# A hybrid decoder trunk on one core: the samples' attention and decays' sums in the norms' rounds, half of the attention's projection ahead of the scan, and tile 1's first two query blocks alone

## What is computed

```
h = RMSNorm(x) * (1 + scale) + shift            # scale, shift: from c @ w_ada (6 vectors of 1024 per sequence)
parts = h @ w_in                                # q, k, v | conv input | decay, beta | z | gate_a, gate_b
A: sliding-window attention (window 128, 8 heads of 64, 2 kv heads, sinks, bias) -> @ w_att_out
B: q, k, v = silu(conv4(...)); q, k = l2norm(q), l2norm(k)       # 4 heads of 128
   g = -exp(a_log) * softplus(decay + dt_bias); beta = sigmoid(...)
   delta rule with decay exp(g), chunk by chunk (128 tokens), gated RMSNorm with silu(z) -> @ w_delta_out
y = sigmoid(gate_a) * A + sigmoid(gate_b) * B;   x += gate1 * RMSNorm(y @ w_out)
h2 = RMSNorm(x) * (1 + scale2) + shift2
query = h2 @ w_query                            # 8 heads x 2 halves of 128
scores against 128 sub keys per half, top 16 of each, top 16 of the 256 sums -> 16 experts of 16384
f = sum over experts of gate * gelu(h2 . u_e) * v_e;   x += gate2 * RMSNorm(f)
```

## Time and profile before

| | |
|---|---|
| median of 3 runs | 1865.48 us (1865.09 to 1865.55) |
| profiled execution | 1861.27 us, of which the span of the trace 1859.5 us |
| TensorE clock granted, mean | 0.83 of full |
| busy: TensorE, VectorE, ScalarE, GpSimd | 1447.3, 1248.9, 704.1, 611.3 us |
| read from memory | 640.84 MB, 348 GB/s over the span |
| gathers | 520, first dot product at 468 us |
| TensorE, VectorE busy from 250 to 462 us | 196.4, 160.0 us |

### The profile page before, as it was taken

One profiled execution on the slowest core, in us unless ns is written; L12 is line 12 of the kernel. 1 busy time (PEld: TensorE's weight loads), 2 busy tenths in 40 slices (PEclk: granted clock), 3 DMA queues, 4 the chain that ended last, 5 costly groups with the idle time before them and its releaser, 6 DMA issues.

```text
span 1859.5 us, 23227 instructions
## 1 busy us (share of the span) xinstructions
PE 1447.3 (78%) x8298; PEld 684.0 (37%) x8298; DVE 1248.9 (67%) x2827; ACT 704.1 (38%) x1799; POOL 611.3 (33%) x590
## 2 busy tenths in 40 slices
PE   8999988999888889689776666666666676667666
PEld 4777877887454446444222111101111110001001
DVE  3077678776866665776767666777667677667665
ACT  3145472213545553935324222432222243222223
POOL 1100000000543323333445444454444444444442
PEclk9999998999999999899988767867766676665666
DMA  9533362126999999999999999999999999999997
GB/s 348 179 121 118 129 241 80 35 80 219 417 421 419 422 414 405 401 342 394 413 420 423 425 424 424 425 424 425 424 424 423 421 423 417 422 421 418 423 422 305
DMA packets 101059, 647.54 MB, mean 348 GB/s; under 512 B 11858, under 2 KB 12026, under 8 KB 32933
## 3 DMA queue, kind: packets, MB, share of 16 engines
q0 software_dynamic: 76912, 555.82, 72.3%
q1 hardware_dynamic: 23840, 90.16, 13.3%
q10 hardware_dynamic: 192, 0.09, 0.0%
HBM read 640.84 MB, written 6.18 MB: 348 GB/s over the span
## 4 chain that ended last, share of the span: by engine, by line
PE 38%; DMA 38%; DVE 9%; ACT 9%; issue 5%; POOL 1%; ACTq 0%; SPq 0%; DVEq 0%; POOLq 0%
DMA arena<-in_euv,consts 37%; PE abank L926 23%; PE dbank L1654 4%; PE dbank L926 4%; DVE arena L2390 3%; PE fsum L1654 2%; PE fsum L1648 2%; ACT consts L892 2%; ACT L890 2%; ACT small L890 1%; ACT L795 1%; DMA arena<-in_wstream 1%; PE fsum L990 1%; POOL arena L480 1%; PE abank L1538 1%
## 5 line engine op out<-in xcount | busy, mean ns | idle before, releaser
L2390 DVE CUSTOM_DVE_ANT_0 arena<-arena 128x1024 f32<-128x1024 f32 x520 | 632.8, 1223 | 387.6 <-DMA arena<-in_euv,consts 386.7
L480 POOL DMA_INDIRECT arena<-in_euv,consts x520 | 577.0, 1110 | 784.3 <-PE dbank L1654 335.5
L926 PE MATMUL abank<-arena 128*128 128x128 f32 (+4 forms) x2456 | 555.1, 383 | 19.5 <-ACT arena L497 6.9
L1654 PE MATMUL dbank<-arena,consts 128*32 128x512 f32 x1024 | 364.5, 850 | 202.2 <-ACT consts L892 201.9
L926 PEld LDWEIGHTS abank<-arena 128*128 128x128 f32 (+1 forms) x2456 | 393.0, 191 | 176.0 <-issue 65.4
L890 ACT ACTIVATE small<-small 128x1 f32<-128x1 f32 x520 | 104.7, 201 | 639.5 <-DVE small L2390 632.9
L1654 PE MATMUL fsum<-arena,consts 128*32 128x512 f32 x512 | 191.2, 873 | 113.9 <-ACT consts L892 113.3
L1654 PEld LDWEIGHTS dbank<-arena,consts 128*32 128x32 f32 x1024 | 42.4, 124 | 487.9 <-ACT consts L892 475.9
L497 ACT ACTIVATE arena<-abank 128x512 f32<-128x512 f32 (+5 forms) x237 | 116.0, 489 | 253.2 <-PE abank L926 240.0
L892 ACT ACTIVATE consts<-arena,small 128x32 f32<-128x32 f32 x520 | 167.1, 321 | 16.9
L1654 PEld LDWEIGHTS fsum<-arena,consts 128*32 128x32 f32 x512 | 21.6, 126 | 263.5 <-ACT consts L892 261.0
(11 more groups left out here) (338 smaller groups left out, 1196.1 us busy)
## 6 DMA issues: line engine op xcount, KB each, us to landing
arena<-in_wstream SPq DMA_DIRECT2D x140, 512.0 KB, 6.2
arena<-in_euv,consts POOLq DMA_INDIRECT x520, 13.2
arena<-in_wout SPq DMA_DIRECT2D x8, 1024.0 KB, 8.8
arena<-in_x SPq DMA_DIRECT2D x5, 512.0 KB, 6.8
arena<-in_sdel POOLq DMA_DIRECT2D x1, 2048.0 KB, 9.1
out_deltas<-arena POOLq DMA_DIRECT2D x1, 2048.0 KB, 12.0
out_yp<-arena SPq DMA_DIRECT2D x4, 512.0 KB
arena<-mod SPq DMA_DIRECT2D x3, 512.0 KB, 10.0
```

Of the source, the lines that this page charges most:

```text
L480: pool.indirect_dma_start(ring[n % SLOTS], None, I["euv"], bass.IndirectOffsetOnAxis(cur[:, u % 2, c:c + 1], 0)).then_inc(ring_in[n % SLOT ...
L926: return pe.matmul(out, lhsT, rhs, start=first, stop=last)
L1654: last = pe.matmul(out[e][to:to + 32, :], weighed, v, start=h == 0 and kk == 0, stop=h == PH - 1 and kk == 3, skip_group_check=True)
L2390: TTR(uh, uh, rep[j] if t < NT else h2sb, 1.0, 0.0, ALU.mult, ALU.add, dot[:, n // NQ % 2, n % NQ:n % NQ + 1]).then_inc(s.dots_done, 1)
```

## The change

It has three parts, and some places that follow from them.

1. Rounds of the norms. `AHEAD` puts three ada blocks in each of the first four rounds and none in the other four. The samples' attention, which stood behind the rounds, is a function `own_attention(m)` of the rounds on TensorE and ScalarE, and its VectorE steps, those of g and the remaining modulation stand in the rounds too. The samples' bias and logits are added in the bank (two products into one) instead of on VectorE. ScalarE makes beta ahead of the rounds.
2. Start of the scan. Two of the four gates left stand right behind the rounds, the other two ahead of decays 1 and 2. Two of the four attended blocks (`N_EARLY`) stand ahead of decays 2 and 3, the other two in levels 2 and 3. VectorE's product of E1 with the triangle is gone in each chunk (the later masks hold it). `mgt` lies elsewhere, so it doesn't wait until the modulation has been written out.
3. Stream. Tile 1 is the first of the later tiles in norm and transpose, then the samples; mixing begins a tick later, norms and transposes two. Query blocks 0 and 1 are done for tile 1 alone, 128 columns, at ticks 51 and 52 (`ALONE`), between the transposes of the samples, of tile 2 and of tile 3. Their columns for the other tiles are done at ticks 76 and 79 with the same blocks loaded a second time, so SyncE's last run of loads has 18 instead of 16 blocks.

The diff, cut to its core:

```diff
-BEHIND, AHEAD = [5, 1, 1, 1] + [1] * B_CONV, [1, 2] * DH
+BEHIND, AHEAD = [5, 1, 1, 1] + [1] * B_CONV, [3] * DH + [0] * DH
 GATES = [("z", m) for m in range(B_Z)] + [("a", m) for m in range(B_GA)] + [("b", m) for m in range(B_GB)]
 ROUNDS = [1, 1, 2, 2, 2, 2, 2, 2]
+N_EARLY = 2
...
-        LATER = [NT, 1, 2, 3]
+        LATER = [1, NT, 2, 3]
...
-        MIX_FROM = 34
+        MIX_FROM = 35
         OD_AT = {3: (0,), 4: (1,), 5: (2, 3), 6: (4,), 7: (5, 6), 8: (7,)}
-        GATE_AT = {i: g for g, i in enumerate((9, 11, 13, 15, 17, 18, 20, 21, 23, 24, 26, 27, 29, 30, 32, 33))}
-        FIRST_AT = {i: PH + m for m, i in enumerate((8, 10, 12, 14, 16, 19, 22, 25))}
-        NORMAL = {45: 0, 46: 1, 47: 2, 48: 3}
-        SECOND = {47: 0, 48: 1, 49: 2, 50: 3}
-        TURN = {48: 0, 49: 1, 50: 2, 51: 3}
-        ROWS_LATER = {53: 1, 55: 2, 57: 3}
-        QUERY_AT = (52, 53, 54, 55, 57, 58, 59, 62, 64, 67, 70, 73, 76, 79, 82, 85)
-        QUERY = {i: m for m, i in enumerate(QUERY_AT)}
-
-        SPREAD = {36: (0, 1), 39: (2, 3), 42: (4, 5), 44: (8,), 56: (6, 7)}
+        GATE_AT = {i: g for g, i in enumerate((9, 11, 13, 15, 17, 18, 20, 21, 23, 25, 26, 28, 29, 31, 32, 34))}
+        FIRST_AT = {i: PH + m for m, i in enumerate((8, 10, 12, 14, 16, 19, 22, 24))}
+        NORMAL = {47: 0, 48: 1, 49: 2, 50: 3}
+        SECOND = {49: 0, 50: 1, 51: 2, 52: 3}
+        TURN = {50: 0, 51: 1, 52: 2, 53: 3}
+        ROWS_LATER = {54: 1, 56: 2, 58: 3}
+        ALONE = {51: 0, 52: 1}
+        QUERY_AT = (54, 55, 57, 58, 59, 62, 65, 68, 71, 74, 76, 79, 83, 86, 89, 92)
+        QUERY = dict(zip(QUERY_AT, list(range(2, 12)) + [0, 1] + list(range(12, 2 * PH))))
+
+        SPREAD = {37: (0, 1), 40: (2, 3), 43: (4, 5), 47: (8,), 63: (6, 7)}
...
-            if QUERY.get(i - 1) == 1:
+            if ALONE.get(i - 1) == 1:
...
-        STREAM = list(range(N_QRY + 8)) + BETWEEN + list(range(N_QRY, N_QRY + B_QRY))
+        STREAM = list(range(N_QRY + 8)) + BETWEEN + [N_QRY + m for m in [0, 1] + list(QUERY.values())]
...
+            act.wait_ge(s.cols_in, 48)
+            step(A(ealog, cols[:, K_ALOG:K_ALOG + 4], ACT.Exp))
+            act.wait_ge(s.gx_ready, 1)
+            step(A(gtmp2, gtmp, ACT.Abs))
+            step(A(gtmp2, gtmp2, ACT.Exp, scale=-1.0))
+            step(A(gtmp2, gtmp2, ACT.Ln, bias=ones[:, 0:1]))
+            step(A(beta, nat[:, :, 260:264], ACT.Sigmoid), s.beta_ready)
...
+            def own_attention(m):
+
+                if m == 1:
+                    for i in range(2):
+                        empty(probT[:, 4 * i:4 * i + 4, :])
+                    act.sem_inc(s.kTs_ready, 1)
+                if m == 2:
+                    for kv in range(2):
+                        empty(lt64.rearrange("p (q v g) -> p q v g", v=2, g=HG)[:, :, kv, :], slice(0, NB * HG), scale=HD ** -0.5)
+                    act.sem_inc(s.lt_ready, 1)
+                if m == 3:
+                    empty(prob[0:64, 0, 0:P], slice(0, P), slice(0, 64))
+                    act.sem_inc(s.own_ready, 1)
+                if m == 5:
+                    act.wait_ge(s.nm_ready, NT + 1)
+                    step(A(prob[0:64, 0, 0:P], prob[0:64, 0, 0:P], ACT.Exp, bias=nm8[0:64, 0:1], accum_out=sm8[0:64, 0:1]))
+                    step(A(es8[0:64, 0:1], es8[0:64, 0:1], ACT.Exp), s.exp_done)
+                if m == 6:
+                    empty(ex, slice(0, 48), func=ACT.Exp)
+                    act.sem_inc(s.ex_ready, 1)
+                if m == 7:
+                    empty(lt64, slice(0, 64))
+                    act.sem_inc(s.lt_ready, 1)
+
             for m in range(2 * DH):
                 if m >= 2:
                     act.wait_ge(s.l2_done, m - 1)
...
+            act.sem_inc(s.att_done, 1)
             act.wait_ge(s.mrows_ready, 8)
             for ch in range(NT):
-                if ch == 2:
-                    b = aring.to_read()
-                    step(A(attT[:, :, SEQ:TOK], b[:, 0:32].rearrange("p (b g) -> p g b", g=HG), ACT.Copy), s.aring_free)
-                    act.sem_inc(s.att_done, 1)
+                if ch in (1, 2):
+                    gates(1)
+                if ch >= NT - N_EARLY:
+                    others_attended(ch - NT + N_EARLY)
...
+            def own_attention(m):
+
+                if m == 1:
+                    pe.wait_ge(s.keyc_in, 16)
+                    for i in range(2):
+                        b = aring.to_fill()
+                        for e in range(4):
+                            last = pe.transpose(b[:, e * P:(e + 1) * P], keyc[:, 4 * i + e, :], ident)
+                        last.then_inc(s.aring_full, 1)
+                if m == 2:
+                    pe.wait_ge(s.kTs_ready, 1)
+                    for kv in range(2):
+                        half = slice(64 * kv, 64 * kv + 64)
+                        b = aring.to_fill()
+                        for q in range(NB):
+                            last = mm(b[:, q * HG:(q + 1) * HG], probT[half, q, :], qT[half, :, SEQ + q])
+                        last.then_inc(s.aring_full, 1)
+                if m == 3:
+                    b = aring.to_fill()
+                    mm(b[0:64, 0:P], rels[:, :], onehot[:, P:2 * P], True, False)
+                    pe.wait_ge(s.lt_ready, 1)
+                    mm(b[0:64, 0:P], lt64, ident, False, True).then_inc(s.aring_full, 1)
+                if m == 6:
+                    pe.wait_ge(s.g_ready, 1)
+                    b = aring.to_fill()
+                    for i, tri in enumerate((le, gt, ones)):
+                        last = mm(b[:, 16 * i:16 * i + 16], tri, gg[:, 0:NT, :])
+                    last.then_inc(s.aring_full, 1)
+                if m == 7:
+                    pe.wait_ge(s.prob_ready, NT + 1)
+                    b = aring.to_fill()
+                    pe.transpose(b[:, 0:64], prob[0:64, 0, 0:P], consts[0:64, 0:64]).then_inc(s.aring_full, 1)
+
...
+            keys_and_values(2)
+            keys_and_values(3)
+            for ch in range(NT):
+                if ch in (1, 2):
+                    gate()
+                if ch >= NT - N_EARLY:
+                    pe.wait_ge(s.att_done, 1)
+                    attended()
+                decays(ch)
...
+            def query_begin(m):
+                lo = P if m < 2 else 0
...
+                if i in ALONE:
+                    pe.wait_ge(s.h2T_ready, 2)
+                    project(h2T[1], ((0, P),))
...
-            for n in range(N_AGAIN + 4, N_AGAIN + B_QRY):
+            for n in range(N_AGAIN + 4, N_AGAIN + B_QRY + 2):
...
-                if m == 1:
-                    for c in range(4, 8):
+                if m in (1, 2, 4, 5):
+                    for c in range(*{1: (4, 6), 2: (6, 8), 4: (8, 10), 5: (10, 12)}[m]):
                         modulation(c)
+                if m == 3:
+                    dve.wait_ge(s.beta_ready, 1)
+                    step(STT(gg, gtmp, 0.0, gtmp2, ALU.max, ALU.add))
+                    step(STT(gg, gg, -1.0, bc(ealog, 1, NT + 1), ALU.mult, ALU.mult), s.g_ready)
+                if m == 4:
+                    dve.wait_ge(s.own_ready, 1)
+                    step(dve.tensor_reduce(mx, q0, AX.X, ALU.max))
+                    step(TT(mx, mx, sink, ALU.max))
+                    step(TT(es, sink, mx, ALU.subtract))
+                    step(TS(nm, mx, -1.0, None, ALU.mult), s.nm_ready)
+                if m == 6:
+                    dve.wait_ge(s.exp_done, NT + 1)
+                    step(TT(sm_, sm_, es, ALU.add))
+                    step(recip(sm_, sm_))
+                    step(TS(q0, q0, sm_, None, ALU.mult), s.prob_ready)
                 if m >= 1:
                     dve.wait_ge(s.rn_ready, m)
...
-                step(TT(e1, e1, bc(gt, 1, DH), ALU.mult))
...
+            if N_EARLY == 2:
+                attended(0)
+            decays(2)
...
+            if N_EARLY:
+                attended(N_EARLY - 1)
```

157 lines of the change are left out of this document (47 added, 110 removed).

## The result

The changed kernel took **1891.55 us** (median of 4 runs, 1889.68 to 1895.73), the kernel before 1865.28 beside it (4 runs): 1.0152 of before, 95% interval 1.0136 to 1.0168. It is slower by some 26 to 28 us, where 8 us faster was forecast, and outside the range (to 1868). The profiled execution of the changed kernel took 1895.73 us (span 1893.9), that of before 1861.27; the two profiles differ by 34.5 us, 8 more than the medians.

What follows compares the result with a forecast made beforehand. It took a chain of engines to bound the first quarter and a stream of 520 gathered blocks the rest. Front -3 and stream -5 took 1865.5 to 1857.5 us; range 1849 to 1868.

Steps and rivals of the forecast that it cites:

- Rounds, "3.8 us later": Rounds of norms: VectorE begins keys and values at 279.9, not 276.12, so 3.8 us later.
- the rival: Slower: TensorE's clock halves after idle spells in rounds 6, 7 and levels 4, 5; two halvings +12, 1869.5 us; chance 0.13.
- The replay: Queues ahead of the stream replayed with durations from the profile's rows; it put the start of keys and values at 279.9.
- the chain for beta, costed at 0.5: ScalarE's 5.2 us for beta, moved ahead of round 1, costs 0.5 us, since TensorE is in a gate of 7.2.
- Decays, "+4.0 at this point, 3.8 of it there already": Start of the scan: last mask at 323.6, second products of level 1 4.0 us later, 3.8 of it from the rounds.
- Levels, "-6.1 to -7.0": Merge levels 4 and 5 without attended blocks: 2.3 to 3.2 us off level 4, 3.8 off level 5.
- Table loads, taken at 1.28 without a drain: ScalarE's five added loads in rounds and decays take 1.28 us each; a drain would cost 7 us more.
- Stream, "-7.5 + 2.5 = -5.0": Gathered blocks: 7.5 us back from the wait for tile 1's first scores, 2.5 for two blocks fetched again; net -5.0.
- the hole: Stream at 800 to 860 us: 344 GB/s against 423, 11.2 us lost, 7.5 of them expected back.
- Gates and first queries up to one tick later ... nothing: Stream: these later places cost nothing, the DMA being the bound there; without cover, one gate of 5.6 us late.
- the queries keep TensorE the bound: Rival for the stream: first scores no sooner, or queries behind them keep TensorE the bound; 1865 us; chance 0.2.
- wrong-if clauses: Prediction is wrong if the first dot product comes after 468 us, or the stretch of the queries stays under 360 GB/s.

Runs made afterwards that it cites:

- Front alone: The kernel before with the change's parts ahead of the stream only, its stream as before: 1877.6 us, 1.0072 of before.
- stream alone: The kernel before with the change's stream part only, its front as before: 1874.6 us, 1.0056 of before.
- the rounds as before: Change's front, stream of before, all four attended blocks in levels 2 to 5, modulation blocks spread over all eight rounds as before: 1869.5 us, 1.0020.
- Filled: Change's front with both early attended blocks, stream of before, plus five matmuls nobody reads in levels 4 and 5: 1878.1 us, 1.0062 of before.
- the version without the shift: Kernel before plus tile 1's first two query blocks alone and two more weight blocks, ticks of before, each tile's own wait: 1860.0 us, 0.9973.

## Why the prediction was wrong, step by step

In the changed kernel's own profile the front's terms came out as +13.4 for the rounds (forecast +3.8), +0.8 for the decays (+0.2) and -2.6 for the levels (-6.1 to -7.0), 11.8 in all with what follows, where -3.0 was forecast.

- **Rounds, "3.8 us later"**: mis-sized; 13.4 in this profile (289.51 less 276.12). Front alone has 10.4 against a profile of before's front that starts as early as its own (284.92 less 274.50, of stream alone). Of the rest 2.5 is a gate at the lower clock behind an idle spell of 2.94, which was in the rival, not in the sum; front alone has the same spell, but its clock stayed at 1.00 and its gate took 3.73. The loss stands in the middle: 16.8 us from the third reciprocal to the fourth, where before has 5.2, front alone 16.7, and the rounds as before 16.3, so it is not the modulation. The replay took the samples' scores, which stand there, at half of the earlier trace rows's 3.58, for the clock: front alone has them at 3.31 with the clock at 1.00. The logits came 5.3 later than forecast. And the chain for beta, costed at 0.5, moved the first norm by 5.9. What each of these is worth by itself no run separates.
- **Decays, "+4.0 at this point, 3.8 of it there already"**: right as a difference. 14.2 at the second products of level 1 against 13.4 at the start of keys and values; VectorE idle 5.84 where some 6 were forecast. But the difference hid the price. The prediction has both ends of it: VectorE's own work would be done at 314.4, and with the two blocks ahead the last mask is at 323.6. These 9.2 us, 10 as measured, were never set against the 6.1 to 7.0 for which they were paid; by the prediction's own figures the move was a loss. (The 318.8 that it compares with is misread: the row runs from 318.13 to 321.0. Work taken away had more to give than it counted.)
- **Levels, "-6.1 to -7.0"**: the step that I called the surest, and wrong. The changed kernel gave 2.6. Front alone gave 3.1 in level 4 (15.2 between merges for 18.3), of which 1.6 was before's own dip of the clock, and level 5 and its last merge took back all but 0.8. The sum was VectorE's own, but the block that went was what kept TensorE busy; its first products at half the clock then paced VectorE. Filled, the levels give 5.8, and 4.1 against a profile of before's front without a dip. The error was to leave the clock to a rival while the sum assumed it held, and to take one profile of before for its usual time.
- **Table loads, taken at 1.28 without a drain**: right. In front alone a load at 264.95 is followed by its activation at 266.25. The Trainium skill (ScalarE: Activation LUTs, What ACT_TABLE_LOAD costs) would add some 1.38 to each; no run here shows it.
- **Stream, "-7.5 + 2.5 = -5.0"**: right in size for what it costed, -5.2, but only in the version without the shift. There the hole closes as said, by 9.8 where 7.5 were forecast, and 4.5 are lost ahead of it that were not costed; that the sum fits is in part luck. What failed is the sentence that the rest lies where the DMA is the bound: "Gates and first queries up to one tick later ... nothing", and the spread and the queries moved without a price. Undone first, the later ticks are worth 6.5, and behind that the spread at 63 3.4 and query 8 at 65 5.4; together with the wait they cost 15 to 16. At tick 64 a query fills the time in which TensorE waits for ScalarE to take tile 0's sums; a tick later it stands ahead of the next product.
- **A wait not read.** The diff turns `ROWS_LATER[i] + 2` into `NT + 1`. I named neither the wait nor what is queued behind it. It was the longest of the stream, 13.55 us. Its price was 3 to 6 us with the later ticks (3 is less than the runs can tell) and nothing without them.
- **The rivals.** The slower one had the right mechanism for the front, worked out at +12 where some 3 were lost in the levels of the changed kernel (5 in front alone) and 2.5 in the rounds, and no place in the stream. That the queries keep TensorE the bound was not what happened. The Trainium skill (TensorE: Matmul & The Clock Gate, What's actually happening) has an idle array at 1.2 GHz; the filled run agrees, 0.50 against 1.00. The dip in level 4 of before, with TensorE busy ahead of it, is not explained by that.

The wrong-if clauses spoke: the first dot product came after 468, and the stretch of the queries stayed at 356 GB/s, under 360.

## What to carry to other kernels

When work leaves the engine that runs a chain's matmuls, price what is left at both clocks in the sum itself; five fillers of 0.95 us in the gaps were worth 3 to 5 us of the chain here (no run shows them in the whole time). Where work is moved from one stretch of a chain to another, work out both stretches with and without it: here 9 us were paid for 7 at best. When a table of places moves, price every moved entry against what waits in its new slot, above all beside a tile's hand-over; and try the idea with the old places first, since here the idea gave 5 us, and its ticks and places took 15. Read every changed wait as a new instruction.

## What the runs showed of the hardware that was not expected

- The same front, in ten profiles of kernels that share it, had its first dot product anywhere from 463.0 to 468.5 us. A shift of 1.4 us stands there before 117 us; most of the rest are two steps of 1.6 us, one between keys and values and level 1's first merge (47.4 or 49.0 us) and one in level 4 or 5 (16.7 or 18.3). A step of 2 us can't be read from one pair of profiles.
- The step in level 4 or 5 goes with TensorE's clock (0.72 in 362 to 368 of before, 1.00 at the same place of stream alone). The trace of before shows next to no idle TensorE ahead of it (busy for 23.89 of 24 us in 326 to 350 and all of 350 to 374), so idle time alone did not tell where the clock falls; what else did is open.
- The samples' scores (64 rows, 4 columns) took 3.31 us for 32 passes with TensorE's clock at 1.00, and 3.58 at 0.50: such small products hardly follow the clock.
- VectorE stood still for 13.2 to 14.0 us at tick 54, and removing the wait gave only 3 to 6 of them.
